# Selected-key attention: values as the stationary operand, two heads to the halves of a bank, weights divided in the scores' step

## The chip, the cores and the metric

One core of one Trainium2 chip runs the whole program in one launch. The metric is the time of one execution on the device in microseconds (us); lower is better.

## The reference

Four blocks run over 512 tokens of 1024 features, all in float32: a dilated-window attention, a differential attention, and then two hybrid layers, each with a mixer and a gated feed-forward part. Only the hybrid mixer is touched. It has a gated linear recurrence, and beside it an attention with 8 heads of 64 features over keys that an indexer chooses (chunks of 64 tokens are causal, at most 128 keys per query):

```python
score = einsum('bqhs,bqh->bqs', relu(dots), w)          # the indexer
score = where(admissible, score, -inf)
top_val, top_idx = lax.top_k(score, topk)               # topk = 128
logits = einsum('bqhd,bqkhd->bhqk', q, k_sel) * 64 ** -0.5
p = softmax(where(valid, logits, -inf))
out = einsum('bhqk,bqkhd->bqhd', p, v_sel)
```

The kernel does not gather. It computes the scores against all keys up to the query's block, adds a large negative number where a key was not chosen, and then takes the softmax. The attention's output goes through the matrix `p_attn`, is gated and added to the recurrence's part.

## The kernel before, in words

**One list of steps.** `Order` writes one list of steps by hand, and each engine (the functions `tensor`, `scalar`, `vector`, `pool`, `sync`) walks the same list and issues its own instructions of every step, in that order. Semaphores, counted ahead in `build`, connect them. So a wait on an engine holds whatever stands behind it in that engine's part of the list.

**Projections.** The weights are streamed in tiles of 1 MB or less. ScalarE rounds a tile to the fast float32r form (line 1995), GpSimd forms the remainder (line 2927), and TensorE multiplies in three passes (lines 1634, 1638, 1641), each product with 512 moving columns. `wide` yields after every 6 products, `feature_major` after every 12 with a weight of 2.

**Side work.** In `hybrid` (lines 666 to 864) a generator of side steps, `side`, runs beside the projections: `beside` takes from it 0.994, 1.147, 1.512 or 0.54 steps (`R0` to `R3`, line 28) per unit that the projections yield. The stretch with 1.147 holds the later projections (`gq`, `gk`, `gv`, `gr`), that with 1.512 the gates b, that with 0.54 the gates a. The side work is in this order: attention and the choice of keys (`choices`, with the decays behind it) in turn, two attention yields to one of the other; then the recurrence (`gla`); then its norm, the turning of its output (`turn` with the tag `o0` or `o1`, two yields each), and last the four steps that bring the attention's output into the layout of the next product (`chunk` with the tag `a0` or `a1`).

**Attention, unit by unit.** A unit n is a query block b (0 to 3) and a head h, 32 per layer; J = b + 1 key blocks. `staged` lines three steps up, so that in each round the result of unit n-2, the turn of unit n-1 and the scores of unit n are issued:

- `scores3` (for two heads at once): TensorE multiplies both heads' queries and keys (line 1862, 64 rows each, banks 4 and 5), VectorE adds the mask and takes the maximum (line 2678), ScalarE the exponential with its sum (line 2215).
- `turn3`: TensorE transposes the J blocks of weights (line 1873) into bank 6 or 7, ScalarE copies them out (line 2224), VectorE takes the reciprocal of the sum (line 2688).
- `out3`: TensorE multiplies with the turned weights as the stationary operand, 128 columns, and the head's values as the moving one, 64 columns (line 1884). VectorE multiplies by the reciprocal while it copies out of the bank (line 2696), into `XA`, tokens by features.

A plain float32 product is two records of TensorE (two loads, two products); a transpose is one. Banks 6 and 7 alternate over all such small steps (`takes_corner`), and each step waits until its bank has been read. The recurrence has a product of a similar kind: `read` (line 1946), 64 stationary columns each to one half of a bank, 256 moving columns.

**Out of the attention.** Each `chunk a` step makes four transposes (line 1712), ScalarE rounds them into `EA` (line 2037), and VectorE forms the remainder (through line 2344, a helper that many operations share). Products with `EA` start with the tile `pa0`.

Of the kernel before, what the change touches and what calls it, by code (L numbers as in the profile page):

```python
# [6 lines left out]
F32 = mybir.dt.float32  # L7
# [172 lines left out]
class Order:  # L180
# [485 lines left out]
    def hybrid(self, l):  # L666
# [67 lines left out]
        def attention():  # L734
            units = att_units()

            def scores(n):
                while "av" not in on or units[n][0] and units[n][0] not in chosen:
                    yield False
                if n % 2 == 0:  # L740
                    self.step("scores3", l, n)
                    yield

            def turn(n):
                self.step("turn3", l, n)
                yield

            def out_of(n):
                self.step("out3", l, n)
                yield  # L750

            yield from self.staged(len(units), [scores, turn, out_of])
# [52 lines left out]
        def gla_norm():  # L805
            while "gr" not in on or "gla" not in on:
                yield

            while complete or not loaded:
                yield from head_norm()  # L810
            for b in range(NB):
                self.step("turn", f"o{l}", b)
                if b == 0:
                    self.step("moments", l, NB - 1)
                yield
                yield
                if b == 1:
                    self.step("gate_o", l, NB - 1)
            while "gb" not in on:
                yield  # L820
            for c in range(4):
                self.step("chunk", f"a{l}", c)
                yield
# [87 lines left out]
def build(nc, ap, out):  # L911
    with ExitStack() as ctx:
# [163 lines left out]
        out_copied = tally("sums_scaled")  # L1076
# [86 lines left out]
        for kind, *a in order.steps:  # L1163
# [31 lines left out]
            elif kind == "chunk":  # L1195
# [3 lines left out]
                freed[k] = chunk_lo.plan(tuple(a))  # L1199
            elif kind == "rope":  # L1200
# [31 lines left out]
            elif kind in ("turn1", "turn2", "turn3"):  # L1232
# [3 lines left out]
                if kind == "turn3":  # L1236
                    recip.plan(key)
# [60 lines left out]
            elif kind == "scores3":  # L1298
# [4 lines left out]
                for e in range(2):  # L1303
                    freed[4 + e] = maxed.plan(("3", l, n + e))
                    exped.plan(("3", l, n + e))
            elif kind == "ranks":
# [207 lines left out]
        XA = arr(0, NB, 512)  # L1514
# [41 lines left out]
        def chunk_io(tag, c, bank):  # L1556
# [4 lines left out]
            d = EA if tag[0] == "a" else AT  # L1561
            return bank[:, :], d[:, 0, c, :], d[:, 1, c, :]
# [21 lines left out]
        def tensor():  # L1584
# [3 lines left out]
            for kind, *a in order.steps:  # L1588
# [112 lines left out]
                elif kind == "chunk":  # L1701
                    tag, c = a
                    if tag in ("l1g", "l2g"):
                        pe.wait_ge(timed.sem, timed.at[index[f"{tag}{c // 2}"], 1])
                        src = X
                    else:
                        pe.wait_ge(out_copied.sem, out_copied.at["3", int(tag[1]), N3 - 1])
                        src = XA
                    k = bank6["chunk", tag, c]
                    pe.wait_ge(*before["chunk", tag, c])  # L1710
                    for b in range(NB):
                        mm = pe.transpose(B[k][:, b * P:b * P + P], src[:, b, c * P:c * P + P], IDN)
# [248 lines left out]
        def scalar():  # L1961
            se = nc.scalar
            for kind, *a in order.steps:
# [56 lines left out]
                elif kind == "chunk":  # L2020
                    tag, c = a
                    src, d, _ = chunk_io(tag, c, B[bank6["chunk", tag, c]])
                    if tag[0] == "a" and c == 0:
                        l = int(tag[1])
                        se.wait_ge(gated_o.sem, gated_o.at[l, NB - 1])
                        for half in range(2):
                            se.wait_ge(spilled[half].sem, spilled[half].at[index[f"m{l}gb3"], half])
                    if tag in ("l1g", "l2g") and c == 0:
# [7 lines left out]
                    else:  # L2036
                        se.activation(d, src, ACT.Copy).then_inc(chunk_hi.sem, 1)

# [168 lines left out]
                elif kind == "scores3":  # L2207
                    l, n = a
                    w = P * (sel_units[n][0] + 1)
                    for e in range(2):  # L2210
                        v = arr(o_p + 512 * e, 512)[:, 0:w]
                        se.wait_ge(maxed.sem, maxed.at["3", l, n + e])
                        if n >= 2:
                            se.wait_ge(recip.sem, recip.at["3", l, n + e - 2])
# [3 lines left out]
                elif kind == "turn3":  # L2218
# [3 lines left out]
                    if n >= 2:  # L2222
                        se.wait_ge(summed.sem, summed.at["3", l, n - 2])
# [115 lines left out]
        def vector():  # L2339
# [7 lines left out]
            for kind, *a in order.steps:  # L2347
# [37 lines left out]
                elif kind == "chunk":  # L2385
# [6 lines left out]
                    else:  # L2392
                        tt(d_lo, src, d_hi.bitcast(F32), ALU.subtract).then_inc(chunk_lo.sem, 1)

# [286 lines left out]

                elif kind == "turn3":
                    l, n = a
                    e = n % 2
                    ve.wait_ge(exped.sem, exped.at["3", l, n])
                    if n >= 2:
                        ve.wait_ge(out_copied.sem, out_copied.at["3", l, n - 2])
                    ve.reciprocal(SM[:, RZ + e:RZ + e + 1], SM[:, ZS + e:ZS + e + 1]).then_inc(recip.sem, 1)

                elif kind == "out3":  # L2690
                    l, n = a
                    b, h = sel_units[n]
                    e = n % 2
                    ve.wait_ge(summed.sem, summed.at["3", l, n])
                    ve.wait_ge(recip.sem, recip.at["3", l, n])
                    ve.tensor_scalar(XA[:, b, h * 64:h * 64 + 64], B[bank6["out", "3", l, n]][:, 0:64],
                                     SM[:, RZ + e:RZ + e + 1], None, ALU.mult).then_inc(out_copied.sem, 1)
# [253 lines left out]
        def sync():  # L2951
# [35 lines left out]
            for kind, *a in order.steps:  # L2987
# [207 lines left out]
```

## Time and profile before

| | |
|---|---|
| runs of the kernel before | 2783.8, 2785.5, 2787.1 us; median 2785.52 |
| the profiled execution | 2781.26 us, its span 2780.0 us |
| TensorE (PE) busy | 2711.5 us, 98% of the span |
| VectorE, ScalarE, GpSimd busy | 43%, 38%, 41% |
| granted clock of TensorE, mean | 0.996 |

The profile shows one execution. Busy times of TensorE overlap, since the next product starts before the last has left the array; so the distance from one start to the next says what a step takes, and the duration of a record is longer than that.

### The profile page before, as it was taken

The numbers are of one execution on the slowest core, as the hardware profiler recorded it, in microseconds if no ns is written. First come the engines' busy times: TensorE is split into PE (matmuls) and PEld (weight loads), VectorE is DVE, ScalarE is ACT, GpSimd is POOL, SyncE is SP. The second block draws the span as 40 slices with busy tenths as digits, with TensorE's granted clock in tenths as the row PEclk, the third lists the DMA queues.
The fourth block names the chain that finished last, engine by engine and source line by source line (L and its number), as shares of the span: only waits on it lengthen the run. The fifth ranks groups of instructions, "written<-read, shape, count | busy, mean of one in ns | idle before, by whom it ended". The sixth has DMA issues, their size and how long they took to land.

```text
span 2780.0 us, 36195 instructions
## 1 busy us (share of the span) xinstructions
PE 2711.5 (98%) x13753; PEld 2181.4 (78%) x13753; DVE 1183.2 (43%) x2435; ACT 1060.5 (38%) x2013; POOL 1135.2 (41%) x894
## 2 busy tenths in 40 slices
PE   8999999999999999999999999999999999999998
PEld 6887878888778877776788888887777678888887
DVE  3434343443564355333236424265533323642425
ACT  3343434353345343363333424234336233342422
POOL 4434343434342443323364444444332236454442
PEclk9999999999999999999999999999999999999999
DMA  5424333432331322223252323323222324333221
GB/s 186 136 87 139 96 118 96 122 130 78 112 89 56 112 91 76 84 87 105 93 176 80 122 91 99 99 81 122 76 84 87 103 84 169 98 109 101 94 93 59
DMA packets 214913, 286.40 MB, mean 103 GB/s; under 512 B 16846, under 2 KB 154546, under 8 KB 213972
## 3 DMA queue, kind: packets, MB, share of 16 engines
q1 hardware_dynamic: 214740, 284.08, 32.3%
q8 instruction: 110, 1.80, 0.3%
q14 instruction: 63, 0.52, 0.1%
HBM read 248.31 MB, written 18.94 MB: 96 GB/s over the span
## 4 chain that ended last, share of the span: by engine, by line
PE 92%; DVE 3%; ACT 2%; issue 1%; POOL 1%; DMA 1%; SPq 0%; DVEq 0%; ACTq 0%
PE banks L1641 36%; PE banks L1638 28%; PE banks L1634 12%; PE banks L1776 2%; PE banks L1659 2%; PE banks L1884 1%; PE banks L1758 1%; PE banks L1674 1%; PE banks L1797 1%; PE banks L1698 1%; PE banks L1932 1%; PE banks L1848 1%; PE banks L1862 1%; PE banks L1819 1%; PE banks L1743 1%
## 5 line engine op out<-in xcount | busy, mean ns | idle before, releaser
L2927 POOL TENSOR_TENSOR WS<-WR,WS 128x512 fp32r<-128x512 f32 (+2 forms) x676 | 851.4, 1292 | 1096.0 <-ACT WS L1995 1096.0
L1641 PE MATMUL banks<-WS,UT 128*128 128x512 f32 (+1 forms) x3696 | 799.8, 366 | 6.5 <-DVE UT L2344 6.5
L1641 PEld LDWEIGHTS banks<-WS,UT 128*128 128x128 f32 x3696 | 605.2, 190 | 131.4 <-issue 34.2
L1638 PE MATMUL banks<-UT,WS 128*128 128x512 f32 (+1 forms) x2832 | 666.1, 393 | 0.7 <-ACT AR L2177 0.7
L1638 PEld LDWEIGHTS banks<-UT,WS 128*128 128x128 f32 (+1 forms) x2832 | 527.5, 188 | 125.2 <-issue 15.6
L1995 ACT ACTIVATE WS<-WR 128x1024 fp32r<-128x1024 f32 (+1 forms) x344 | 333.0, 1018 | 223.6 <-PE banks L1641 153.6
L1634 PE MATMUL banks<-UT,WS 128*128 128x512 f32 x1536 | 372.6, 396 | 0.0
L1634 PEld LDWEIGHTS banks<-UT,WS 128*128 128x128 f32 x1536 | 282.2, 188 | 64.6 <-issue 6.2
L1641 PE MATMUL banks<-WS,AT 128*128 128x512 f32 x1296 | 308.2, 396 | 0.0
L1641 PEld LDWEIGHTS banks<-WS,AT 128*128 128x128 f32 x1296 | 242.7, 188 | 58.3 <-ACT WS L1995 0.7
L2925 POOL TENSOR_TENSOR WS<-WR,WS 128x512 fp32r<-128x512 f32 x128 | 180.9, 1444 | 260.0 <-ACT WS L1991 260.0
L2344 DVE TENSOR_TENSOR AF<-banks,AF 128x512 f32<-128x512 f32 x128 | 94.2, 788 | 220.1 <-PE banks L1634 220.1
L2942 POOL TENSOR_TENSOR SM<-SM 128x1 f32<-128x1 f32 (+2 forms) x44 | 45.4, 1031 | 271.2 <-DVE SM L2834 98.9
L2862 DVE SCALAR_TENSOR_TENSOR AR<-banks,AR 128x511 f32<-128x511 f32 x84 | 63.0, 750 | 217.6 <-ACT AR L2313 217.6
L2344 DVE TENSOR_TENSOR AR<-AR,banks 128x512 f32<-128x512 f32 x64 | 43.0, 685 | 168.3 <-PE banks L1641 168.3
L2344 DVE TENSOR_TENSOR AR<-AR 128x512 f32<-128x512 f32 (+3 forms) x93 | 98.0, 1054 | 23.2 <-ACT AR L2065 12.7
L2313 ACT ACTIVATE AR<-banks,AR 128x512 f32<-128x512 f32 x84 | 65.0, 773 | 86.4 <-PE banks L1638 80.3
L2441 DVE CUSTOM_DVE_ANT_0 AF<-banks,MF 128x256 f32<-128x256 f32 (+1 forms) x128 | 46.7, 403 | 104.1 <-PE banks L1743 88.0
L1638 PE MATMUL banks<-AT,WS 128*128 128x512 f32 x384 | 88.2, 391 | 0.0
L1991 ACT ACTIVATE WS<-WR 128x512 fp32r<-128x512 f32 x128 | 69.8, 620 | 41.7 <-PE banks L1634 41.7
L1638 PEld LDWEIGHTS banks<-AT,WS 128*128 128x128 f32 x384 | 72.1, 188 | 15.8
L2086 ACT ACTIVATE AF<-banks 128x512 f32<-128x512 f32 (+1 forms) x64 | 36.6, 572 | 110.7 <-PE banks L1758 110.7
(224 smaller groups left out, 2709.0 us busy)
## 6 DMA issues: line engine op xcount, KB each, us to landing
WR<-in_w_in SPq DMA_DIRECT2D x112, 512.0 KB, 3.4
WR<-in_w_up SPq DMA_DIRECT2D x88, 512.0 KB, 3.5
WR<-in_dil_w_in SPq DMA_DIRECT2D x64, 512.0 KB, 3.9
WR<-in_w_down SPq DMA_DIRECT2D x40, 512.0 KB, 3.7
WR<-in_diff_w_in SPq DMA_DIRECT2D x32, 512.0 KB, 3.7
WR<-in_dil_w_in SPq DMA_DIRECT2D x32, 256.0 KB, 3.1
AR<-AF SPq DMA_DIRECT2D x128, 64.0 KB, 2.3
AR<-AF SPq DMA_DIRECT2D x64, 128.0 KB, 2.4
```

The source lines that it names most:

```text
L1634: mm = pe.matmul(B[bank][:, :], slot(i, part)[:, c:c + P], act[:, other, kk, :], start=start, stop=stop)
L1638: mm = pe.matmul(B[bank][0:c, :], w[part][:, kk, g * P:g * P + c], act[:, other, kk, :], start=start, stop=stop)
L1641: mm = pe.matmul(B[bank][:, off:off + n], act[:, other, before_k + kk, g * P:g * P + P], w[part][:, kk, :], start=start, stop=stop)
L1659: mm = pe.matmul(B[c][:, 256 * half:256 * half + 256], w[x][:, kk, (c % 2) * P:(c % 2) * P + P], UT[:, y, kk, 256 * half:256 * half + 256] ...
L1776: mm = pe.matmul(B[ob][:, r:r + 64], fat(7168 + 512 * e + 256 * hh + j * P, P), vj, start=(j == 0), stop=(j == w // P - 1))
L1991: x = se.activation(slot(i, 0)[:, to].rearrange("p (a f c) -> p a f c", f=2, c=32), src, ACT.Copy)
L1995: se.activation(slot(i, 0)[:, v * h:v * h + h], raw(i)[:, v * h:v * h + h], ACT.Copy).then_inc(hi.sem, 1)
L2313: se.activation(d, B[order.bank[i, half][0]][:, :], ACT.Identity, scale=cp[:, 2, f:f + 1], bias=cp[:, 3, f:f + 1]).then_inc(conv_id.sem, 1)
L2344: return ve.tensor_tensor(out_, x, y, op)
L2862: ve.scalar_tensor_tensor(d[:, 1:T], bank[:, 0:T - 1], cp[:, 1, f:f + 1], d[:, 1:T], ALU.mult, ALU.add).then_inc(dve_step, 1)
L2925: ge.tensor_tensor(low, src, high.bitcast(F32), ALU.subtract).then_inc(lo_p.sem, 1)
L2927: ge.tensor_tensor(slot(i, 1)[:, s], raw(i)[:, s], slot(i, 0)[:, s].bitcast(F32), ALU.subtract).then_inc(lo_p.sem, 1)
```

## The change

The result product swaps its operands: the values of a head (64 columns) are stationary, and the turned weights (128 columns) move. One step makes two heads, in turn for each key block, to partitions 0 to 63 and 64 to 127 of one bank. The result comes out by features, as the next product wants it, and VectorE copies it into `XA`, which now is features by tokens. Because the sums of the softmax now lie along the free dimension, the weights are divided by their sums before they are turned: reciprocal and scaling stand on VectorE in the step of the scores. The transposes of the `chunk a` steps go; the steps `parts` in their place only round and take the remainder. Every other `out3` step, with its yield, goes.

```diff
@@ Order.hybrid
             def out_of(n):
-                self.step("out3", l, n)
-                yield
+                if n % 2:
+                    self.step("out3", l, n)
+                    yield
             for c in range(4):
-                self.step("chunk", f"a{l}", c)
+                self.step("parts", f"a{l}", c)
                 yield
@@ build
-        XA = arr(0, NB, 512)
+        XA = arr(0, 4, T)
@@ tensor
                 elif kind == "turn3":
-                    pe.wait_ge(exped.sem, exped.at["3", l, n])
+                    pe.wait_ge(weights_scaled.sem, weights_scaled.at["3", l, n])
                 elif kind == "out3":
                     l, n = a
                     b, h = sel_units[n]
-                    e = n % 2
                     pe.wait_ge(pt_out.sem, pt_out.at["3", l, n])
                     for j in range(b + 1):
-                        mm = pe.matmul(B[ob][:, 0:64], arr(o_pt + 512 * e + j * P, P), av[:, j, h * 64:h * 64 + 64],
-                                       start=(j == 0), stop=(j == b))
+                        for e in range(2):
+                            o = (h - 1 + e) * 64
+                            mm = pe.matmul(B[ob][64 * e:64 * e + 64, 0:P], av[:, j, o:o + 64],
+                                           arr(o_pt + 512 * e + j * P, P), start=(j == 0), stop=(j == b))
@@ scalar
+                elif kind == "parts":
+                    tag, c = a
+                    if c == 0:
+                        se.wait_ge(out_copied.sem, out_copied.at["3", l, N3 - 1])
...
+                    se.activation(EA[:, 0, c, :], XA[:, c, :], ACT.Copy).then_inc(chunk_hi.sem, 1)
                 elif kind == "scores3":
                         if n >= 2:
-                            se.wait_ge(recip.sem, recip.at["3", l, n + e - 2])
+                            se.wait_ge(weights_scaled.sem, weights_scaled.at["3", l, n + e - 2])
                 elif kind == "turn3":
                     if n >= 2:
-                        se.wait_ge(summed.sem, summed.at["3", l, n - 2])
+                        se.wait_ge(summed.sem, summed.at["3", l, n - 2 | 1])
@@ vector
+                elif kind == "parts":
+                    tag, c = a
+                    ve.wait_ge(chunk_hi.sem, chunk_hi.at[tag, c])
+                    tt(EA[:, 1, c, :], XA[:, c, :], EA[:, 0, c, :].bitcast(F32), ALU.subtract).then_inc(chunk_lo.sem, 1)
                 elif kind == "scores3":
...
+                    for e in range(2):
+                        v = arr(o_p + 512 * e, w)
+                        ve.wait_ge(exped.sem, exped.at["3", l, n + e])
+                        if n >= 2:
+                            ve.wait_ge(weights_scaled.sem, weights_scaled.at["3", l, n + e - 2])
+                        ve.reciprocal(SM[:, RZ + e:RZ + e + 1], SM[:, ZS + e:ZS + e + 1]).then_inc(recip.sem, 1)
+                        ve.wait_ge(recip.sem, recip.at["3", l, n + e])
+                        ve.tensor_scalar(v, v, SM[:, RZ + e:RZ + e + 1], None,
+                                         ALU.mult).then_inc(weights_scaled.sem, 1)
-                elif kind == "turn3":
-                    ve.wait_ge(exped.sem, exped.at["3", l, n])
-                    ve.reciprocal(SM[:, RZ + e:RZ + e + 1], SM[:, ZS + e:ZS + e + 1]).then_inc(recip.sem, 1)
                 elif kind == "out3":
-                    ve.tensor_scalar(XA[:, b, h * 64:h * 64 + 64], B[bank6["out", "3", l, n]][:, 0:64],
-                                     SM[:, RZ + e:RZ + e + 1], None, ALU.mult).then_inc(out_copied.sem, 1)
+                    ve.tensor_copy(XA[:, h // 2, b * P:b * P + P],
+                                   B[bank6["out", "3", l, n]][:, 0:P]).then_inc(out_copied.sem, 1)
@@ sync
                 elif kind == "load_h":
-                    sy.wait_ge(chunked.sem, chunked.at[f"a{l}", 3])
+                    sy.wait_ge(chunk_lo.sem, chunk_lo.at[f"a{l}", 3])
```

## Rows read from the trace of the kernel before

**Rows 1.** The page: busy times by engine, and the chain by engine.
```profile
PE 2711.5 (98%) x13753; PEld 2181.4 (78%) x13753; DVE 1183.2 (43%) x2435; ACT 1060.5 (38%) x2013; POOL 1135.2 (41%) x894
PE 92%; DVE 3%; ACT 2%; issue 1%; POOL 1%; DMA 1%; SPq 0%; DVEq 0%; ACTq 0%
```
**Rows 2.** Groups by form, weight loads: busy us, mean ns, idle before, releaser.
```profile
L1884 PEld LDWEIGHTS banks<-AR 128*128 128x128 f32 x320 | 44.1, 190 | 19.6 <-ACT AR L2224 11.1 <-issue 4.5
L1946 PEld LDWEIGHTS banks<-AR,AF 128*64 128x64 f32 x128 | 6.5, 135 | 10.5 <-issue 9.5 <-DVE AR L2732 0.7
```
**Rows 3.** Timeline of PE, attention with J=2 and J=4: start, us, instruction.
```profile
1147.08 0.55 PE L1884 MATMUL banks<-AR 128*128 128x64 f32 x4
1147.44 1.63 PE L1641 MATMUL banks<-WS,UT 128*128 128x512 f32 x6
1148.91 0.38 PE L1873 MATMUL banks<-CT,AR 128*128 128x128 f32 x2
...
1150.88 3.01 PE L1641 MATMUL banks<-WS,UT 128*128 128x512 f32 x12
1153.73 0.38 PE L1873 MATMUL banks<-CT,AR 128*128 128x128 f32 x2
...
1240.14 1.00 PE L1884 MATMUL banks<-AR 128*128 128x64 f32 x8
1240.95 1.63 PE L1641 MATMUL banks<-WS,UT 128*128 128x512 f32 x6
```
**Rows 4.** Timeline of PE, the recurrence's reading product (line 1946).
```profile
1282.97 3.01 PE L1638 MATMUL banks<-UT,WS 128*128 128x512 f32 x12
1285.91 0.65 PE L1946 MATMUL banks<-AR,AF 128*64 128x256 f32 x4
1286.50 0.70 PE L1932 MATMUL banks<-AF 64*128 64x256 f32 x4
...
1331.87 1.08 PE L1946 MATMUL banks<-AR,AF 128*64 128x256 f32 x8
```
**Rows 5.** Who waited for whom, PE alone: us, times, longest.
```profile
PE banks L1884 <- ACT AR L2224: 8.1, 10, 1.3
PE banks L1932 <- DVE AR L2732: 6.6, 10, 1.1
...
PE banks L1873 <- ACT AR L2215: 2.2, 2, 1.2
```
**Rows 6.** Timeline of PE, a turn and the result right behind it, J=3.
```profile
1174.13 0.49 PE L1873 MATMUL banks<-CT,AR 128*128 128x128 f32 x3
1175.36 0.88 PE L1884 MATMUL banks<-AR 128*128 128x64 f32 x6 [0.74 <-ACT AR L2224]
```
**Rows 7.** Timeline, scores with J=4 and the end of their first exponential.
```profile
1223.46 1.13 PE L1862 MATMUL banks<-AR 64*128 64x512 f32 x4
...
1226.00 0.18 ACT L2215 ACTIVATION_READ_ACCUMULATOR AR<-AR,SM 128x1 f32 x1
```
**Rows 8.** VectorE: the reciprocal (groups), a scaling in SBUF (one line's instructions, min/median/max ns).
```profile
L2688 DVE RECIPROCAL SM<-SM 128x1 f32<-128x1 f32 x64 | 9.9, 154 | 1.2 <-ACT AR L2215 1.0
...
L2666 DVE TENSOR_SCALAR AR<-AR x6: 280/374/1176, 1034.2 to 2069.8; 128x256 f32<-128x256 f32 x2, 128x384 f32<-128x384 f32 x2, 128x512 f32<-128x512 f32 x2
```
**Rows 9.** Timeline, the first turn of the recurrence's output and its low halves.
```profile
1333.10 1.06 PE L1698 MATMUL banks<-CT,AR 128*128 128x128 f32 x8
...
1334.39 1.29 DVE L2344 TENSOR_TENSOR AT<-banks,AT 128x512 fp32r<-128x512 f32 x2 [0.55 <-ACT AT L2016]
```
**Rows 10.** Timeline of PE, steps `chunk a` and the projections behind the last.
```profile
1361.71 0.60 PE L1712 MATMUL banks<-CT,AR 128*128 128x128 f32 x4
1362.07 3.00 PE L1638 MATMUL banks<-UT,WS 128*128 128x512 f32 x12
...
1368.44 13.87 PE L1638 MATMUL banks<-UT,WS 128*128 128x512 f32 x60
```
**Rows 11.** Stretches: engines' busy us, granted clock, DMA share, GB/s.
```profile
1264.00:1268.00 4.00, 4.00 (x10) 2.44 (x10) 0.69 (x1) 0.71 (x2) 0.00 (x0) 0.57 0.00 0
```

More of the change, by code:

```diff
@@ L1075, in build @@
         negated = tally("max_negated")
-        out_copied = tally("sums_scaled")
+        out_copied = tally("sums_copied")
+        weights_scaled = tally("weights_scaled")
         weighed = tally("weighed")
@@ L1199, in build @@
                 freed[k] = chunk_lo.plan(tuple(a))
+            elif kind == "parts":
+                chunk_hi.plan(tuple(a))
+                chunk_lo.plan(tuple(a))
             elif kind == "rope":
@@ L1235, in build @@
                 pturned.plan(key)
-                if kind == "turn3":
-                    recip.plan(key)
                 freed[k] = pt_out.plan(key)
@@ L1305, in build @@
                     exped.plan(("3", l, n + e))
+                    recip.plan(("3", l, n + e))
+                    weights_scaled.plan(("3", l, n + e))
             elif kind == "ranks":
@@ L1560, in chunk_io @@
                         AT[:, 1, c, :].rearrange("p (l r) -> p r l", r=4))
-            d = EA if tag[0] == "a" else AT
-            return bank[:, :], d[:, 0, c, :], d[:, 1, c, :]
+            return bank[:, :], AT[:, 0, c, :], AT[:, 1, c, :]
         def width1(n):
@@ L1702, in tensor @@
                     tag, c = a
[L1703 to L1708, printed above, removed]
+                    pe.wait_ge(timed.sem, timed.at[index[f"{tag}{c // 2}"], 1])
                     k = bank6["chunk", tag, c]
@@ L1711, in tensor @@
                     for b in range(NB):
-                        mm = pe.transpose(B[k][:, b * P:b * P + P], src[:, b, c * P:c * P + P], IDN)
+                        mm = pe.transpose(B[k][:, b * P:b * P + P], X[:, b, c * P:c * P + P], IDN)
                     mm.then_inc(chunked.sem, 1)
@@ L2022, in scalar @@
                     src, d, _ = chunk_io(tag, c, B[bank6["chunk", tag, c]])
[L2023 to L2028, printed above, removed]
+                    if c == 0:
                         for name in "qk":
@@ L2037, in scalar @@
                         se.activation(d, src, ACT.Copy).then_inc(chunk_hi.sem, 1)
+                elif kind == "parts":
+                    tag, c = a
+                    l = int(tag[1])
+                    if c == 0:
+                        se.wait_ge(out_copied.sem, out_copied.at["3", l, N3 - 1])
+                        se.wait_ge(gated_o.sem, gated_o.at[l, NB - 1])
+                        for half in range(2):
+                            se.wait_ge(spilled[half].sem, spilled[half].at[index[f"m{l}gb3"], half])
+                    se.activation(EA[:, 0, c, :], XA[:, c, :], ACT.Copy).then_inc(chunk_hi.sem, 1)
                 elif kind == "pairs":
@@ L2393, in vector @@
                         tt(d_lo, src, d_hi.bitcast(F32), ALU.subtract).then_inc(chunk_lo.sem, 1)
+                elif kind == "parts":
+                    tag, c = a
+                    ve.wait_ge(chunk_hi.sem, chunk_hi.at[tag, c])
+                    tt(EA[:, 1, c, :], XA[:, c, :], EA[:, 0, c, :].bitcast(F32), ALU.subtract).then_inc(chunk_lo.sem, 1)
                 elif kind == "rope":
@@ L2680, in vector @@
                                                 ALU.min, SM[:, MX + e:MX + e + 1]).then_inc(maxed.sem, 1)
-                elif kind == "turn3":
-                    l, n = a
-                    e = n % 2
-                    ve.wait_ge(exped.sem, exped.at["3", l, n])
-                    if n >= 2:
-                        ve.wait_ge(out_copied.sem, out_copied.at["3", l, n - 2])
-                    ve.reciprocal(SM[:, RZ + e:RZ + e + 1], SM[:, ZS + e:ZS + e + 1]).then_inc(recip.sem, 1)
+                    for e in range(2):
[7 more added lines that the diff above has]
+                                         ALU.mult).then_inc(weights_scaled.sem, 1)
                 elif kind == "out3":
@@ L2692, in vector @@
                     b, h = sel_units[n]
-                    e = n % 2
                     ve.wait_ge(summed.sem, summed.at["3", l, n])
-                    ve.wait_ge(recip.sem, recip.at["3", l, n])
-                    ve.tensor_scalar(XA[:, b, h * 64:h * 64 + 64], B[bank6["out", "3", l, n]][:, 0:64],
-                                     SM[:, RZ + e:RZ + e + 1], None, ALU.mult).then_inc(out_copied.sem, 1)
+                    ve.tensor_copy(XA[:, h // 2, b * P:b * P + P],
+                                   B[bank6["out", "3", l, n]][:, 0:P]).then_inc(out_copied.sem, 1)
                 elif kind == "decay":
```

## The prediction

> **What bounds the kernel now.** I read the busy times first, then the chain that ended last: TensorE is busy for 98% of the span and holds 92% of that chain [rows 1]. So the time is TensorE's stream of instructions, plus the moments in which it stands still. An edit on VectorE or ScalarE counts only if TensorE waits for it. Then I read TensorE's timeline where the changed steps lie (about 1065 to 1260 us for the first hybrid layer, the same again in the second layer) and priced each step by its **slot**: from its start to the next start, plus what the projection products beside it lose by the interruption. Twelve projection products with a 6-product run taken off show one at 0.23 us: a run of 12 takes 1153.73 - 1150.88 = 2.85, a run of 6 takes 1148.91 - 1147.44 = 1.47, so 1.38 for 6, and each run loses about 0.09 to the step behind it [rows 3].
>
> Below, J is the number of key blocks of a step (1 to 4). A plain float32 product leaves two records per product.
>
> **1. The result products.** Before: one step per head, 2J records. J=2 takes 1147.44 - 1147.08 = 0.36, J=4 takes 1240.95 - 1240.14 = 0.81 [rows 3]; with the 0.09 they are 0.45 and 0.90, so 0.225 J. Per layer 8 heads x 0.225 x (1+2+3+4) = 18.0, for two layers 36.0 us. Each record moves only 64 columns but stands for 0.11 us, so it is the loading of 128 stationary columns that sets it.
>
> After: one step per two heads, 4J records that hold 64 columns and move 128, alternately to the two halves of a bank. Nothing of just this form is in the trace. The nearest is the recurrence's reading product (line 1946): 128x64 stationary, two halves of a bank, 256 moving columns. Four records of it take 1286.50 - 1285.91 = 0.59, and the 12 products before it 1285.91 - 1282.97 = 2.94, some 0.18 over 12 x 0.23: 0.77 in all. Eight of them in a row take 0.43 more than four (1.08 against 0.65 of busy time) [rows 4]. Two records of each half thus cost 0.43, where plain products with 512 columns move one at 0.23: 256 columns in both passes of float32 are 0.21, so the two halves run side by side, and the fixed part is 0.77 - 0.43 = 0.34. Halving the columns gives 0.215 per J: a step is 0.34 + 0.215 J, 0.56 / 0.77 / 0.99 / 1.20, times 4 and 2 layers: 28.1 us. **Term: -7.9 us.** Its bounds: if the halves do not overlap, 0.34 + 0.43 J, together 45.3, +9.3. If the fixed part shrinks behind the scores step (often the neighbour, itself in halves), some 0.1 x 32 = 3 better: -11.
>
> The rule that speaks against this: the Trainium skill, TensorE: Matmul & The Clock Gate, Part 3, says that a weight load overlaps a running product only where the row groups differ. Both halves here use all 128 rows, so by it each load of 0.135 us [rows 2] after the first pair would stand open: 128 x 0.135 = 17 us, and the sum at the end would be about 0 instead of -17. The eight records in 1.08 us [rows 4] speak against it.
>
> **2. The turning of the result.** Four steps of four transposes per layer go. One is 1362.07 - 1361.71 = 0.36 [rows 10] plus 0.09, eight of them 3.6 us. The copy and subtraction that follow now read from memory; they run on ScalarE and VectorE while at least 13 us of projections are left before the first product that needs them [rows 10], so I cost them at nothing. **Term: -3.6.** SP's load_h waits for the last of them, which is done long before that step.
>
> **3. Waits for the turned weights.** Now a head's result product comes one step after its transposes, with at most one ScalarE copy between, and it waits: 10 times, 8.1 us on PE [rows 5], 11.1 us by the weight loads [rows 2]. One such pair [rows 6]: transposes at 1174.13, result at 1175.36, where 0.24 would do. After the change the order is result of the pair before, turn, turn, scores of the next pair, result: the scores (about 1.1 us) always lie between. I take 9.6 as what is lost now and leave 0.6. **Term: -9.0**, bounds -6 to -11.
>
> **4. The new chain ahead of the turn.** A turn waited for the exponential; now for a reciprocal and a scaling of 128 x up to 512 behind it: 0.15 + 0.37 [rows 8] and two handovers of about 0.1, some 0.7 us more. At J=4 the scores start at 1223.46 and the first exponential with its sum ends at 1226.18 [rows 7], 2.7 us on; with the chain 3.4. The first turn stands three steps behind the scores wherever the choice of keys or the decays run beside it: at least 1.06 (scores) + 1.2 (result) + two runs of 6 (2.8) = 5.1 us. Slack 1.6. It fails only where ScalarE is held by a 2 us split or a table load; today the turns wait twice in all, for 2.2 us [rows 5]. VectorE also holds the queue through both exponentials, some 3 us per pair: behind it stand the top-8 steps, the adding of the dots and the copy of the result, for which the third turn's bank waits, five steps later. The scaling adds 64 x 0.35 = 22 us to VectorE and the merged copies take 9 away; VectorE is 43% busy. **Term: +1**, bounds 0 to +8.
>
> **5. What moves.** 16 side steps fewer per layer, so all that follows the attention starts about 14 runs of 6 products earlier. A dozen steps of the recurrence leave the stretch with three side steps per 12 products for one with about one per 6: each loses neighbours (+1), and its waits for the state (6.6 us in 10 waits today [rows 5]) get fewer (-1). Then the turning of the recurrence's output, today one step in five runs, falls into the stretch with three per 12. A turn of 8 transposes takes 0.8, and its low half leaves the second bank only at 1334.39 + 1.29, 2.6 us after it started at 1333.10 [rows 9]; another turn right behind must wait up to 1.6 us. I expect one or two such pairs per layer, and a wait for the last block's gate (which passes POOL): **+4**, bounds 0 to +8. SP's load of the gate rows waits for the spilled ones right behind their projection, up to 5 us with the next weights behind it; ScalarE's splits wait for TensorE there, so there is slack. The half clock after the totals (0.57 in 1264 to 1268 [rows 11]) costs 1.7 us; in other company it may go or last longer: 0, give or take 4 for both layers.
>
> **Sum**: -7.9 - 3.6 - 9.0 + 1 + 4 = -15.5 us. Against the profiled execution of 2781.3 that is 2765.8. The median of the runs shown lies 4.3 above it, so for the median I forecast 2785.5 - 15.5 = **2770 us**.
>
> **Rivals.**
> A. *The scaling ends last at every pair.* The first turn of each pair arrives before its weights are scaled. Price 0.7 us x 32 pairs = 22 us, 2792 us: slower. It decides from 0.5 us per pair on. For it: VectorE now waits inside its queue, and in the stretch with J=4 it shares ScalarE with the decays and their table loads. Against: a slack of 1.6 us, two waits today. Chance 0.09.
> B. *The halves don't overlap,* or each load stands open: term 1 turns from -7.9 to about +9, the sum to +1.5, 2787 us. The eight records speak against it. Chance 0.08.
> C. *The waits only change place:* terms 1 and 2 come, but turns, dots and the recurrence's turns take back the 9 us of term 3: -6 to -7, 2779 us. Chance 0.10.
>
> That the change doesn't do what it says can be excluded: order and operands are written out.
>
> **The numbers.** My forecast (2758 to 2777) has 0.73. Down: -11 for terms 1 and 3 each, no cost in term 5 and the clock dip gone gives -27. Up: rival C is inside, of B half. Range 2759 to 2785. About 0.2% (5.6 us) is what a measurement of this kernel can tell from no change: faster 0.83 (forecast and C), same 0.07 (most of B), slower 0.10.
>
> **What would show it.** The result line has 320 records of 128x64 by 128, its PE busy time near 28 us instead of 44, and no wait for the turned weights. Transposes of the a-chunks are gone. The turn waits for VectorE's scaling, under 4 us in all. The recurrence starts before the projections turn to weights-stationary. If the turn's wait is over 15 us, rival A; if a step with J=4 takes over 1.8 us, rival B; if the output's turns wait over 6 us, term 5 was too small.

## The result: slower, and the profile after

The kernel after takes **2800.4 us** (median of 4 runs, 2796.2 to 2802.1), the one before 2785.4; the ratio is 1.0049, 95% interval 1.0036 to 1.0062. The forecast was 2770, its range ended at 2785. The profiled execution took 2801.4 with a span of 2800.1, against 2780.0.

The page of the kernel after, busy times and chain by engine:

```profile
PE 2717.5 (97%) x13721; PEld 2168.7 (77%) x13721; DVE 1225.3 (44%) x2467; ACT 1060.7 (38%) x2013; POOL 1138.9 (41%) x894
PE 90%; DVE 4%; ACT 3%; issue 2%; DMA 1%; POOL 1%; SPq 0%; DVEq 0%; ACTq 0%
```

Against [rows 1], TensorE has lost 32 records and is busy 6 us longer, and it holds 90% of the chain instead of 92%: both waits and slower records have come. The groups by form say what became of the changed steps (busy us, mean ns, idle before):

```profile
L1884 PE MATMUL banks<-AR 128*64 128x128 f32 x320 | 24.5, 283 | 3.6 <-ACT AR L2229 3.6
L1884 PEld LDWEIGHTS banks<-AR 128*64 128x64 f32 x320 | 16.8, 136 | 15.9 <-issue 11.4 <-ACT AR L2229 4.4
L2772 DVE TENSOR_SCALAR AR<-AR,SM 128x256 f32<-128x256 f32 x24 | 19.8, 886 | 6.8 <-POOL SM L2951 6.8
L2698 DVE TENSOR_SCALAR AR<-AR,SM 128x128 f32<-128x128 f32 x16 | 11.8, 735 | 0.6
...
L2698 DVE TENSOR_SCALAR AR<-AR,SM 128x512 f32<-128x512 f32 x16 | 7.8, 486 | 0.6
```

The line of the result product in the kernel before, for comparison:

```profile
L1884 PE MATMUL banks<-AR 128*128 128x64 f32 x320 | 44.4, 269 | 8.1 <-ACT AR L2224 8.1
```

The result product is what was forecast: 320 records of 128x64 by 128, 24.5 us busy where it was 44.4, its loads 16.8 where they were 44.1 [rows 2], and 3.6 us of waits where there were 8.1 [rows 5]. Two lines are odd. The scaling of 128 columns (line 2698) takes longer than that of 512. And line 2772, which scales the recurrence's output and is not touched by the change, takes 886 ns a piece. The timeline of PE gives the slots of the new result step, J=1 and J=4:

```profile
1102.51 1.66 PE L1645 MATMUL banks<-WS,UT 128*128 128x512 f32 x6
1104.10 0.44 PE L1884 MATMUL banks<-AR 128*64 128x128 f32 x4
1104.47 1.68 PE L1645 MATMUL banks<-WS,UT 128*128 128x512 f32 x6
...
1198.95 1.64 PE L1645 MATMUL banks<-WS,UT 128*128 128x512 f32 x6
1200.52 1.09 PE L1884 MATMUL banks<-AR 128*64 128x128 f32 x16
1201.54 1.66 PE L1645 MATMUL banks<-WS,UT 128*128 128x512 f32 x6
```

J=1: 0.37, and the run of 6 ahead of it takes 1.59 instead of 1.38, together 0.58. J=4: 1.02 + 0.19 = 1.21. The prediction had 0.56 and 1.20.

So the loss lies elsewhere. Who waited for whom, PE alone (us, times, longest):

```profile
PE banks L1932 <- DVE AR L2741: 11.2, 10, 2.9
...
PE banks L1872 <- DVE AR L2698: 5.2, 4, 2.4
PE banks L1912 <- DVE AR L2349: 5.0, 2, 2.5
...
PE banks L1702 <- DVE AT L2349: 3.7, 4, 1.1
PE banks L1884 <- ACT AR L2229: 3.6, 2, 1.8
...
PE banks L1932 <- ACT AR L2265: 2.1, 2, 1.0
```

The waits for the state (line 1932) have doubled, from 6.6 [rows 5] to 11.2 + 2.1. The totals of the decays (line 1912), 32 products with 2 moving columns each, and the turns of the recurrence's output (line 1702, for `AT`) waited for nothing before; nor did the results (line 1884) wait 1.8 us at once. Here is the totals' wait, the timeline of all engines in the first hybrid layer:

```profile
1238.24 1.12 PE L1902 MATMUL banks<-MF,AR 17*128 17x512 f32 x2
1239.30 2.59 PEld L1645 LDWEIGHTS banks<-WS,UT 128*128 128x128 f32 x12 [0.76 <-issue]
...
1240.02 1.28 ACT L2248 ACT_TABLE_LOAD   x1
...
1241.97 1.28 ACT L2250 ACT_TABLE_LOAD   x1
1243.26 0.63 ACT L2250 ACTIVATE AR<-AR 128x512 f32<-128x512 f32 x1
...
1243.99 0.69 DVE L2349 TENSOR_TENSOR AR<-AR 128x512 f32<-128x512 f32 x1 [3.27 <-ACT AR L2250]
1244.80 6.90 PEld L1912 LDWEIGHTS banks<-CT,AR 128*128 128x128 f32 x32 [2.91 <-issue]
1244.83 6.96 PE L1912 MATMUL banks<-CT,AR 128*128 128x2 f32 x32 [2.52 <-DVE AR L2349]
```

The last decay step (line 1902) is now the last of the side steps ahead of the recurrence. Its chain through ScalarE, with two table loads, and VectorE ends at 1244.68, 6.4 us after the product began; one run of 12 is all that lies between. And the totals take 6.96 us. The same place before, timeline of PE:

```profile
1228.38 1.12 PE L1902 MATMUL banks<-MF,AR 17*128 17x512 f32 x2
...
1259.36 1.00 PE L1884 MATMUL banks<-AR 128*128 128x64 f32 x8
1260.19 3.69 PE L1912 MATMUL banks<-CT,AR 128*128 128x2 f32 x32
```

There the last decay lay 31.8 us back, with 14 attention yields behind it, and the totals took 3.69. The stretches (engines' busy us, granted clock, DMA share, GB/s) of the kernel after tell why they now take twice as long in this layer:

```profile
1244.00:1250.00 6.00, 5.17 (x25) 5.20 (x25) 0.68 (x1) 1.19 (x1) 0.00 (x0) 0.55 0.00 0
1250.00:1256.00 6.00, 6.00 (x20) 4.77 (x20) 0.00 (x0) 0.55 (x2) 0.00 (x0) 0.60 0.00 0
```

Behind the wait TensorE's clock is at 1.2 GHz instead of 2.4 for some 10 us (0.45 x 6 + 0.40 x 6 = 5.1 us of full clock lost). Before, 0.57 in 4 us was all in this layer [rows 11]. The second layer has the same wait of 2.5 us and not the same loss. Its totals and the stretch around them, after:

```profile
2160.49 4.88 PE L1912 MATMUL banks<-CT,AR 128*128 128x2 f32 x32 [2.52 <-DVE AR L2349]
2162.00:2170.00 8.00, 8.00 (x30) 6.36 (x30) 0.00 (x0) 0.37 (x2) 0.00 (x0) 0.57 0.00 0
```

And before, with no wait in front:

```profile
2166.18 4.78 PE L1912 MATMUL banks<-CT,AR 128*128 128x2 f32 x32
2168.00:2176.00 8.00, 8.00 (x28) 6.25 (x28) 0.69 (x1) 0.80 (x2) 0.00 (x0) 0.57 0.20 62
```

There both kernels lose the same 0.43 x 8 = 3.4 us of full clock.

### The profile page after: what moved, and what is told of

Same layout as the page of the kernel before. It is cut to its first block, busy times and chain, and to the rows that moved or that the text cites. A ratio compares the mean times of both kernels' runs of the same rounds, so it can differ in the third digit from the quotient of the medians.

```text
span 2800.1 us, 36059 instructions
## 1 busy us (share of the span) xinstructions
PE 2717.5 (97%) x13721; PEld 2168.7 (77%) x13721; DVE 1225.3 (44%) x2467; ACT 1060.7 (38%) x2013; POOL 1138.9 (41%) x894
## 4 chain that ended last, share of the span: by engine, by line
PE 90%; DVE 4%; ACT 3%; issue 2%; DMA 1%; POOL 1%; SPq 0%; DVEq 0%; ACTq 0%
PE banks L1645 37%; PE banks L1642 27%; PE banks L1638 12%; PE banks L1775 2%; PE banks L1663 2%; PE banks L1757 1%; PE banks L1678 1%; PE banks L1796 1%; PE banks L1861 1%; PE banks L1884 1%; ACT WS L1995 1%; DVE AR L2349 1%; PE banks L1847 1%; PE banks L1932 1%; PE banks L1818 1%
## 5 line engine op out<-in xcount | busy, mean ns | idle before, releaser
L1991 ACT ACTIVATE WS<-WR 128x512 fp32r<-128x512 f32 x128 | 69.8, 620 | 44.1 <-PE banks L1638 44.1
```

What stands on the lines that cost most here:

```text
L1991: x = se.activation(slot(i, 0)[:, to].rearrange("p (a f c) -> p a f c", f=2, c=32), src, ACT.Copy)
```

## The experiments

The theory: the edits on the steps (terms 1 to 4) gain what was forecast, and the side steps that went (term 5) cost it all, since the recurrence comes too early. The rivals: the chain of the scaling costs it, or the clock does so whatever the order.

**Pace given back.** The kernel after, where each unit yields again, with or without a step:

```diff
                 if n % 2:
                     self.step("out3", l, n)
-                    yield
+                yield
```

> The changed kernel, but the result step yields as often as before (80 attention yields a layer again, 16 of them with nothing in them), so that the recurrence and the steps behind it come as late as before. Theory S (the change's own terms are right; the loss comes from side steps that moved 16 places ahead, wait, and drop the clock): faster than before by 10 to 20 us, about 2768, half clock in the two changed stretches back to about 10 us from 37.6. Rival V (VectorE's longer step in the scores, with its waits inside the queue, costs the time): within 5 us of the changed kernel, about 2798.

Measured: **2766.9 us** (5 runs), 0.9933 (0.9919 to 0.9946) of the kernel before. That is 18.8 below before and 33.5 below after; 32 empty yields are the whole difference. The waits of PE on the changed places:

```profile
PE banks L1932 <- DVE AR L2741: 6.6, 10, 1.1
PE banks L1872 <- DVE AR L2698: 5.7, 4, 2.4
```

The totals, results and output turns no longer wait, and the state is back at its 6.6. The time at half clock in the two changed stretches came back to 17.1 us, not to the 10 that were expected.

**The pace alone, on the kernel before.** Nothing else is changed:

```diff
                 self.step("out3", l, n)
-                yield
+                if n % 2:
+                    yield
```

> The kernel before, but the result step of every even unit doesn't yield, so that 16 yields a layer go and nothing else changes (same products, same scaling, same transposes). Theory S: slower than before by 10 to 30 us, with a wait before the totals and more half clock. Rival V: within 3 us of before, since no VectorE work was added.

Measured: **2807.0 us**, 1.0074 (1.0061 to 1.0086): +21 us, with the old steps and no scaling. Its waits of PE are those of the kernel after (lines 1933, 1913, 1699: state, totals, output turns):

```profile
PE banks L1933 <- DVE AR L2733: 11.2, 10, 2.9
...
PE banks L1913 <- DVE AR L2345: 5.4, 2, 2.9
...
PE banks L1699 <- DVE AT L2345: 3.7, 4, 1.1
```

The same 32 yields cost 33.5 us in the kernel after. Part of the difference is the results' waits: here they fall from 8.1 to 4.4 us, there they rise from 0 to 3.6.

**No scaling.** The kernel after without the division by the sums: the scaling of the weights is left out, and the turns wait for the exponential alone.

```diff
-                    pe.wait_ge(weights_scaled.sem, weights_scaled.at["3", l, n])
+                    pe.wait_ge(exped.sem, exped.at["3", l, n])
...
-                        ve.tensor_scalar(v, v, SM[:, RZ + e:RZ + e + 1], None,
-                                         ALU.mult).then_inc(weights_scaled.sem, 1)
```

> The changed kernel without the scaling of the weights by the reciprocal of their sums (the division is left out); the turn waits for the exponential alone. Theory S: 2 to 8 us faster than the changed kernel (the turn's waits of 5.2 us go, and one spell of half clock per layer), still 2790 or more. Rival V: most of the loss goes, 2785 or less.

Measured: **2794.7 us**, 5.7 below after, with intervals that overlap (1.0021 to 1.0046 against 1.0036 to 1.0062); the turns' waits go from 5.2 to 2.2. The scaling costs some 6 us here at most and is not what made the kernel slower than before: without it the kernel still is.

**Where the empty steps have to be.** The kernel after with 16, then with 4, empty yields ahead of the recurrence, and with 16 behind it (the line `gla()` is moved above them):

```diff
             yield from self.both(attention(), choices())
+            for _ in range(16):
+                yield
             yield from gla()
```

> The changed kernel with 16 empty yields between the end of the attention and decays and the beginning of the recurrence. Theory S: the waits before the totals, for the state and for the turns of the output go back to what they were before: 2766 to 2776. Rival V: as the changed kernel, about 2798. Against e1: if the attention's own steps profit from the slower pace too, e1 is the faster of the two, by up to 4 us.

> The changed kernel with 4 empty yields between the end of the decays and the recurrence, in place of the 16 of e4. The decays' chain on ScalarE and VectorE is then done before the totals, but the recurrence still comes 12 side steps too early. Theory: the wait before the totals (5.0 us) and the two or three spells of half clock that it brings go, 8 to 12 us under the changed kernel (2788 to 2792), and the waits for the state (13 us, with VectorE's scalings held up by GpSimd) stay. Rival (the early recurrence is harmless, the totals are all of it): 2775 or less.

> The changed kernel with the 16 empty yields between the recurrence and the turning of its output. The wait before the totals and the early recurrence stay, the turns of the output come as late as before. Theory: most of the loss sits before and inside the recurrence (waits for the totals 5 us, for the state 6.7 us more, half clock with them), only 3.7 us of waits in the output's turns: 2785 to 2795. Rival (the output's turns are the costly part): 2775 or less.

Measured: 16 ahead **2767.5 us**, 4 ahead **2776.9** (11 runs, 2774.2 to 2782.0), 16 behind **2793.6** (7 runs, 2787.1 to 2799.1). Ahead they give back all; behind the recurrence some 7 us, by intervals that overlap (1.0018 to 1.0041 against 1.0036 to 1.0062). Four give 23.5 of 33.5 us, or 21.6 if each is taken against the kernel before in its own comparison: the theory's 2788 to 2792 was wrong, since I had taken the waits for the state to stay. The rival, that the totals are all of it, isn't shown either. With four, the waits of PE are (lines 1704 and 1934: output turns, state):

```profile
PE banks L1704 <- DVE AT L2351: 7.4, 2, 3.7
...
PE banks L1934 <- DVE AR L2743: 4.4, 8, 0.6
```

The totals don't wait, and run at full clock, timeline of PE in the first layer:

```profile
1238.82 7.09 PE L1647 MATMUL banks<-WS,UT 128*128 128x512 f32 x30
1245.75 3.63 PE L1914 MATMUL banks<-CT,AR 128*128 128x2 f32 x32
```

They start 0.9 us later than in the kernel after and end 2.4 us earlier (1249.38 against 1251.79). The state's waits fall to 4.4, below those of the kernel before, and the 24 head scalings of the recurrence's output (its line 2774) take 410 ns on average, not 886: where a step of the recurrence falls among the projections decides it, not how early it comes. So these four yields take away more than the wait for the totals: 5.0 us there, 8.9 at the state, and the half clock of 20.4 us, against 3.7 more at the output turns. What stays against 16 yields is a turn that waits 3.7 us once a layer.

**Term 3 alone.** The kernel before, with the results of two heads in one step, operands as before, every yield kept (the semaphores and VectorE's two scalings out of the bank follow it):

```diff
-                self.step("out3", l, n)
+                if n % 2:
+                    self.step("out3", l, n)
                 yield
...
-                    for j in range(b + 1):
-                        mm = pe.matmul(B[ob][:, 0:64], arr(o_pt + 512 * e + j * P, P), av[:, j, h * 64:h * 64 + 64],
-                                       start=(j == 0), stop=(j == b))
+                    for e in range(2):
+                        for j in range(b + 1):
+                            o = (h - 1 + e) * 64
+                            mm = pe.matmul(B[ob][:, 64 * e:64 * e + 64], arr(o_pt + 512 * e + j * P, P), av[:, j, o:o + 64],
+                                           start=(j == 0), stop=(j == b))
```

> The kernel before, with the results of two heads in one step (every odd unit; the even unit keeps its empty yield), operands not swapped, scaling and transposes as before. It does term 3 of the prediction alone. Theory: the waits of the result for the turned weights (8.1 us on PE) go and nothing else changes: 2776 to 2779, 7 to 10 us under before. Rival: the waits only move (to the turns or the banks): 2783 or more.

Measured: **2776.0 us** (2768.9 to 2778.6), 0.9965 (0.9953 to 0.9978): 9.0 below the kernel before, by the interval 6 to 13. Nothing waits for turned weights in its profile.

**The first turn of a layer, and who scales.** In the kernel after with its pace given back, the turns still wait 5.7 us, 2.4 of it at one turn of each layer. The timeline of the kernel after shows that turn:

```profile
1068.94 4.97 POOL L2936 TENSOR_TENSOR WS<-WR,WS 128x512 fp32r<-128x512 f32 x4 [3.10 <-ACT WS L1995]
...
1069.93 0.49 PE L1861 MATMUL banks<-AR 64*128 64x128 f32 x4
...
1071.33 0.16 DVE L2696 RECIPROCAL SM<-SM 128x1 f32<-128x1 f32 x1 [0.35 <-ACT AR L2220]
...
1071.53 1.23 DVE L2698 TENSOR_SCALAR AR<-AR,SM 128x128 f32<-128x128 f32 x1
...
1072.81 0.33 PE L1872 MATMUL banks<-CT,AR 128*128 128x128 f32 x1 [2.39 <-DVE AR L2698]
```

No result step and no other side work stands between the first scores and the first turn, and the scaling of 128 columns takes 1.23 us while GpSimd runs four instructions of 1.24 each. Two edits on top of e1_pace, first two yields ahead of that turn:

```diff
             def turn(n):
+                if n == 0:
+                    yield
+                    yield
                 self.step("turn3", l, n)
```

> e1 with two more empty yields between the first scores of a layer and their turn. Theory: the first turn's two waits of 2.4 us go and the spell of half clock behind one of them (1.7 us): 4 to 7 us under e1, about 2761. Rival (the wait comes again at the next turn or elsewhere): within 2 us of e1.

Then the scaling by ScalarE in place of VectorE:

```diff
+                    for e in range(2):
+                        v = arr(o_p + 512 * e, 512)[:, 0:w]
+                        se.wait_ge(recip.sem, recip.at["3", l, n + e])
+                        se.activation(v, v, ACT.Copy, scale=SM[:, RZ + e:RZ + e + 1]).then_inc(weights_scaled.sem, 1)
...
-                        ve.tensor_scalar(v, v, SM[:, RZ + e:RZ + e + 1], None,
-                                         ALU.mult).then_inc(weights_scaled.sem, 1)
```

> e1 with the scaling of the weights on ScalarE in place of VectorE; the reciprocal stays on VectorE. Theory P (VectorE's scaling stands still while a GpSimd instruction of 1.29 us runs, which is why it took 1.23 us for 128 columns): the scaling takes 0.4 to 0.7 us by width without a spread, the turns wait less than in e1 (5.7 us) by 1 to 3 us: 2763 to 2767. Rival (the spread has another cause, or ScalarE's queue is what counts): the turns wait as long or longer, 2767 or more.

And both, with the two yields taken from units 0 and 2, so that the attention keeps its length:

```diff
                 if n % 2:
                     self.step("out3", l, n)
+                if n % 2 or n > 2:
                     yield
```

> e8 (scaling on ScalarE, old pace) with two empty yields between the first scores of a layer and their turn, taken from the empty yields of the first two units, so that all that follows keeps its place. Theory: the first turn's waits (3.5 us) go and do not come again at the tail as in e7: 2759 to 2763. Rival: another step of that length waits in its place: 2764 or more.

Measured: **2768.2 us** for the two yields, no gain over 2766.9: the waits of the first turns are gone, but the attention ends two yields later, and other turns and results wait there. The waits of PE for the scaling (line 1875 is the turn) add up to what they were, and the results wait 1.5 us anew:

```profile
PE banks L1875 <- DVE AR L2701: 5.8, 4, 2.2
```

The scaling on ScalarE gives **2765.1 us** (2762.6 to 2769.4), which its interval (0.9918 to 0.9942) doesn't tell from e1_pace; its turns wait 3.5 us, 2 times. Both together give **2761.2 us** (2758.6 to 2765.1), 0.9915 (0.9901 to 0.9928) of the kernel before: the lowest median here, and 22 us below the kernel before, which had 2783.6 in that comparison; its interval still overlaps those of e1_pace and e8_act_scale. Its turns wait 0.3 us in all, groups by form:

```profile
L1876 PE MATMUL banks<-CT,AR 128*128 128x128 f32 x160 | 28.5, 276 | 0.3
```

**All traces side by side.** Us, both layers together, from one profile each. The first column is the length of the two stretches from the first scores to the first product with `EA`; then the waits of PE there (the rows of the waits); last how long the trace has the clock at half there. A us at half clock is counted as half a us lost.

```
                      stretch  totals  state  turns  results  out turns  half clock
before                  634.4     0     6.6    2.2     8.1        0         10.2
after                   649.6    5.0   13.3    5.2     3.6       3.7        37.5
e1_pace                 617.9     0     6.6    5.7      0         0         17.1
e2_shift                655.5    5.4   13.3    3.5     4.4       3.7        30.7
e3_unscaled             643.2    5.0   13.3    2.2     3.6       3.7        30.7
e4_pad                  618.3     0     6.6    5.3     3.6        0         10.2
e5_merged               621.2     0     6.6    2.2      0         0          6.8
e6_pad_late             638.7    5.0   13.3    5.2     3.6        0         23.9
e7_first                617.6     0     7.2    5.8     1.5        0         13.7
e8_act_scale            613.9     0     6.6    3.5      0         0         10.2
e9_pad4                 626.6     0     4.4    5.3     3.6       7.4        17.1
e10_both                611.4     0     6.6    0.3      0         0         10.2
```

After against e1_pace: the stretches are 31.7 us longer. The waits are 30.8 - 12.3 = 18.5 of it, the half clock 20.4 / 2 = 10.2, and 3.0 are left over. The same sum for e9_pad4 against e1_pace gives 20.7 - 12.3 = 8.4 of waits and no clock, where 8.7 was measured; for e6_pad_late 14.8 + 3.4 = 18.2 of 20.8.

The clock of one profile is one execution's, and it varies from run to run: the profiled ones of e2_shift, e5_merged and e6_pad_late are the fastest of their kernels, those of e4_pad and e10_both the slowest. The mean granted clock of all runs gives, as time lost, 25.9 us after (4 runs), 15.5 in e1_pace (5 runs) and 14.2 before (9 runs): 10.4 between the first two, as in the sum above. It does not bear out a difference between after and e3_unscaled (25.9 and 25.7), and their whole profiles have the same half clock, 55.2 and 55.0 us. So of the 5.7 us of the scaling in e3_unscaled, 3.0 are waits, and the rest has no cause shown.

## Why the prediction was wrong

**Term 1 (-7.9) was right.** The slots are 0.58 and 1.21 for J=1 and J=4 against 0.56 and 1.20 forecast: the halves run side by side. Rival B would have 1.8 or more at J=4, and it is refuted. So is, for this form, the rule of the Trainium skill (TensorE: Matmul & The Clock Gate, Part 3) that a weight load overlaps a running product only where the row groups differ. Sixteen loads of 0.136 would alone be 2.2 us; the 16 records with their loads took 1.02, and both halves use all 128 rows. The same section also lets the load into a background weight buffer run ahead; no run here shows what is at work. The rule, read as the prediction read it, fails for the projections too: 12 products in 2.85 us [rows 3], each with a load of 0.19 us (mean of line 1641) over all 128 rows. The prediction's sum by this rule has two slips: it counts 128 loads, half of the 256 behind the first pair of each step, without a reason, and its -17 for the sum is -15.5 by its own terms.

**Terms 2 and 3 (-3.6, -9.0) were right.** Merging alone measured -9.0 (-6 to -13, so the digit is luck); the transposes of the a-chunks are gone, and the copies in their place are waited for by nobody.

**Term 4 (+1) was too small**, by 2.5 us of waits with the pace given back (turns 5.7 against 2.2); in the kernel after, leaving the scaling out was worth 5.7 us, 3.0 of it waits and the rest unexplained. "The first turn stands three steps behind the scores" doesn't hold for the first pair of a layer: there is no result of a pair before to stand between. And the 0.37 for a scaling was the median of [rows 8], whose maximum, 1176 ns for the same operation, I did not follow up: the scalings of the change that ran beside GpSimd took as long. Rival A, this at every pair, did not come: 4 waits.

**Together**, terms 1 to 4 were forecast at -19.5 us, and with the pace given back the kernel measured -18.8. Terms 1 and 2 have no run of their own, and term 4 was 2.5 us too small, so that the sum fits this closely is in part luck.

**Term 5 (+4, bounds 0 to +8) is the step that failed: it was +33.5.** It took the moved recurrence to wait no more than before and priced the turns of its output alone. Three parts of it were wrong, and a fourth was left out: the results wait 3.6 us where the kernel with its pace has none.

- *The totals.* I went through the recurrence's own waits and those behind it, but not through the first step behind the attention. The decays run beside the attention of the last block. Fourteen attention yields used to follow the last decay; with 16 fewer it is the decay that ends last, and the totals need it at once: 2.5 us per layer.
- *The state.* I wrote that its waits "get fewer (-1)"; they doubled. Running earlier, the head scalings of the recurrence's output meet GpSimd's remainders. Timeline of the kernel after:

```profile
1318.48 5.14 POOL L2936 TENSOR_TENSOR WS<-WR,WS 128x512 fp32r<-128x512 f32 x4
1318.55 5.22 DVE L2772 TENSOR_SCALAR AR<-AR,SM 128x256 f32<-128x256 f32 x4 [1.12 <-POOL SM L2951]
...
1324.94 0.99 DVE L2741 SCALAR_TENSOR_TENSOR AR<-AR,SM,banks 128x256 f32<-128x256 f32 x2
...
1326.04 0.81 PE L1932 MATMUL banks<-AF 64*128 64x256 f32 x4 [2.91 <-DVE AR L2741]
```

  Four scalings take 5.22 us, the update of the state (line 2741) stands behind them on VectorE, and TensorE waits 2.91 for it. In the kernel before none of the 24 took more than 416 ns. All profiles bear this out: in the four with 13.3 us of waits for the state (after, e2_shift, e3_unscaled, e6_pad_late) these scalings take 886 ns on average, in the other eight, with 4.4 to 7.2 us of waits, 407 to 410.
- *The clock.* I put it at 0, give or take 4. In the stretches it cost (37.5 - 10.2) / 2 = 13.7 us more than before, as much as the new waits. Of the 27.3 us more at half clock, 6.8 lie at the first turns, 6.8 at the totals and 13.7 in the recurrence, near its waits for the state. But that a wait brings half clock with it isn't shown, as the last section says, and no run changed one wait alone.

The output turns I had expected: "over 6 us" would have meant that term 5 was too small; they waited 3.7. I had looked for the loss there, at the end of the moved work, and most of it lay before: 5.0 us of waits at the totals and 6.7 more at the state. Rival C (the waits only change place) named the turns, the dots and the turns of the output, neither the totals nor the state, and stopped at 2779 us; no rival had the moved recurrence as a loss beyond 8 us.

**What stays open.** In the profile of the kernel after the clock also falls in code that is the same in both kernels. A stretch of after:

```profile
345.00:352.00 7.00, 6.31 (x27) 5.08 (x26) 3.99 (x12) 3.25 (x8) 2.67 (x2) 0.76 0.25 92
```

In before it has 1.00. The part up to the first scores is 4.0 us longer after (1069.9 against 1065.9). Such dips, up to 600 us, stand in the profiles of all eight kernels made from the one after, e1_pace with its 1068.8 too, and in none of the two made from the one before. Why a change in the hybrid layers should move them is not settled. So of the 15 us between before and after a part of up to 4 has no cause shown; of the 33.5 us of term 5, measured against e1_pace, only 1.1 lies there. Why the clock falls at one wait and not at its like is open as well.

## What to carry to other kernels

In a hand-written interleave a yield is a resource of its own. An edit that removes steps moves everything behind them, and its price is read by walking the list again from the point of removal: for each of the next steps, what is the last chain it needs, and how much work lies between now. The cheap test is to make the edit with the yields kept, and to take them away as a second change; here the first was worth -19 us and the second +33. The granted clock moved with the order too, by some 10 us here, but not wait by wait: take it from several runs and not from one profile.

## What the runs showed of the hardware

**VectorE stands still for GpSimd.** The scaling within SBUF has one input from memory and one scalar per partition, yet it is held while a GpSimd instruction with two inputs from memory runs. In the kernel after, the 16 scalings of 128 columns fall into 8 of about 286 ns and 8 with GpSimd busy, of 908 to 1412; line 2772 into 12 of 409 and 12 of 1345 to 1382. A copy of the same 128 columns out of a bank took 286 on average, 32 times. The Trainium skill (SBUF — State Buffer, Who interferes with whom) has the mechanism, a port pair that one of the two engines holds for a whole instruction, and names this operation among those that can take it; the trace agrees, with four scalings in 5.22 beside four GpSimd instructions in 5.14. On ScalarE the scaling takes longer when nothing interferes (394 ns for 128 columns, 708 for 512), but nothing holds it: in e8_act_scale those beside a GpSimd instruction took 386 to 403 ns for 128 columns, those alone 385 to 403.

**A short wait was followed by half clock at one place and not at the next.** In the first layer of the kernel after, the wait of 2.5 us ahead of the 32 products with 2 moving columns was followed by about 10 us at 1.2 GHz, in which they took 6.96 us instead of 3.63. In the second layer the same wait was followed by 6.8 us, and they took 4.88 us; in the kernel before they took 4.78 there, with no wait, and 6.8 us at half clock followed as well. The first turn's wait of 2.4 us in the first layer has a granted clock of 0.83 around it:

```profile
1070.00:1076.00 6.00, 3.61 (x15) 2.79 (x15) 3.38 (x9) 1.16 (x5) 3.92 (x4) 0.83 0.44 125
1076.00:1080.00 4.00, 4.00 (x17) 3.09 (x15) 0.00 (x0) 0.77 (x2) 0.00 (x0) 0.83 0.19 74
```

That is 10 x 0.17 = 1.7 us lost. In e1_pace the same wait has this in the first layer (1072.1 to 1075.5), and in the second (1970.93) the clock stays at 1.00. In e6_pad_late both waits of 2.9 us for the state leave it at 1.00, where in the kernel after 3.4 and 6.8 us at half clock stand beside them. What lowers it is thus not the wait alone; no run here settles what is.
